# Two PSUM banks for the last projections and four for the level steps of a two-level attention layer

## The reference, cut to what matters

```python
q = silu(q); g = lb + (1 - lb) * sigmoid(f); k = 1 - g
b = cumsum(log(g))                       # within a chunk of tokens, per head and key
a[t, s] = sum_d q[t,d] * exp(b[t,d] - b[s,d]) * k[s,d]     # only s <= t
o = a @ i + (what earlier chunks left in the state)
o = rms_norm(o) * silu(gate);  y = o @ c_w_out
```

## Time and profile before

| | us |
|---|---|
| median of 3 runs | 1267.08 (1266.88 to 1267.08) |
| the profiled execution, its own time | 1267.41 |
| its span, first to last instruction | 1265.6 |
| PE busy | 1250.7 (99%) |
| DVE busy | 986.0 (78%) |
| ACT busy | 747.9 (59%) |
| DMA queue of the weights, share of 16 engines | 51.6% |

### The profile page before, as it was taken

How to read it: one execution, slowest core, us unless ns; L and a number is a source line. 1 busy time by engine, 2 the same in 40 slices (tenths; PEclk the granted TensorE clock), 3 DMA queues, 4 the chain that set the end, 5 groups by cost and what they waited for, 6 DMA issues and landing times.

```text
span 1265.6 us, 22039 instructions
## 1 busy us (share of the span) xinstructions
PE 1250.7 (99%) x8384; PEld 1095.7 (87%) x8384; DVE 986.0 (78%) x1476; ACT 747.9 (59%) x1135; POOL 17.8 (1%) x34
## 2 busy tenths in 40 slices
PE   9999999999999999999999999999999999999997
PEld 7898888888999988888888888888889897888886
DVE  5997899889798879998987676767676665867665
ACT  6565665555888766565557556444445645644443
POOL 0200000000000010000000000000000000000000
PEclk9999999999999999999999999999999999999999
DMA  9754555655544357555536344555655443655551
GB/s 297 262 167 150 183 167 199 199 196 170 167 134 143 127 185 261 200 178 189 199 104 222 118 139 154 200 183 184 198 194 172 134 146 121 216 183 184 199 195 38
DMA packets 165816, 223.16 MB, mean 176 GB/s; under 512 B 5224, under 2 KB 144624, under 8 KB 165616
## 3 DMA queue, kind: packets, MB, share of 16 engines
q1 hardware_dynamic: 163408, 216.04, 51.6%
q0 software_dynamic: 1904, 5.47, 1.3%
q10 hardware_dynamic: 432, 0.64, 0.1%
HBM read 221.08 MB, written 1.06 MB: 176 GB/s over the span
## 4 chain that ended last, share of the span: by engine, by line
PE 89%; DVE 5%; ACT 3%; issue 1%; DMA 1%; SPq 0%; DVEq 0%; ACTq 0%
PE bank L615 24%; PE bank L404 15%; PE bank L405 14%; PE bank L406 14%; PE bank L618 12%; DVE wlow L1707 1%; PE bank L709 1%; PE bank L745 1%; ACT whigh L1205 1%; PE bank L462 1%; PE bank L731 1%; PE bank L524 1%; DMA raw<-in_ab_w_in 1%; PE bank L465 1%; DVE h_e L2164 1%
## 5 line engine op out<-in xcount | busy, mean ns | idle before, releaser
L1707 DVE TENSOR_TENSOR wlow<-raw,whigh 128x2048 fp32r<-128x2048 f32 (+1 forms) x203 | 462.5, 2281 | 132.9 <-ACT whigh L1205 132.6
L1205 ACT ACTIVATE whigh<-raw 128x2048 fp32r<-128x2048 f32 x202 | 386.2, 1912 | 225.2 <-PE bank L406 144.9
L615 PE MATMUL bank<-xn,whigh 128*128 128x512 f32 x1312 | 328.1, 392 | 0.0
L615 PEld LDWEIGHTS bank<-xn,whigh 128*128 128x128 f32 x1312 | 238.1, 189 | 44.2
L618 PEld LDWEIGHTS bank<-xn,wlow 128*128 128x128 f32 x1312 | 179.0, 190 | 12.8
L618 PE MATMUL bank<-xn,wlow 128*128 128x256 f32 x1312 | 182.9, 282 | 0.0
L404 PE MATMUL bank<-xn,whigh 128*128 128x256 f32 (+1 forms) x496 | 142.6, 288 | 0.2 <-DVE f_mk L2287 0.2
L405 PE MATMUL bank<-xn,whigh 128*128 128x256 f32 (+1 forms) x496 | 140.2, 283 | 0.0
L406 PE MATMUL bank<-xn,wlow 128*128 128x256 f32 (+1 forms) x496 | 140.2, 283 | 0.0
L404 PE MATMUL bank<-whigh,g_high 128*128 128x512 f32 (+1 forms) x356 | 138.6, 389 | 0.2 <-DVE g_low L1903 0.2
L405 PE MATMUL bank<-wlow,g_high 128*128 128x512 f32 (+1 forms) x356 | 138.1, 388 | 0.0
(11 more groups left out here) (305 smaller groups left out, 1723.3 us busy)
## 6 DMA issues: line engine op xcount, KB each, us to landing
raw<-in_ffn_w_up SPq DMA_DIRECT2D x44, 1024.0 KB, 5.1
raw<-in_w_gate_up SPq DMA_DIRECT2D x44, 1024.0 KB, 5.0
raw<-in_ffn_w_down SPq DMA_DIRECT2D x22, 1024.0 KB, 4.9
raw<-in_w_down SPq DMA_DIRECT2D x22, 1024.0 KB, 4.9
raw<-in_c_w_in SPq DMA_DIRECT2D x16, 1024.0 KB, 5.6
raw<-in_ab_w_in SPq DMA_DIRECT2D x14, 1024.0 KB, 6.5
raw<-in_w_in_fox SPq DMA_DIRECT2D x10, 1024.0 KB, 5.3
raw<-in_w_in_moba SPq DMA_DIRECT2D x10, 1024.0 KB, 5.1
```

The lines of the kernel that those rows point to most:

```text
L615: pe.matmul(o[:, :].rearrange("p (h t) -> p h t", h=2), wh[:, k, j * P:(j + 1) * P], xn[:, :, k, :], start=k == 0, stop=False)
L1205: act.activation(whigh[s][:, 0:w], raw[s][:, 0:w], ACT.Copy).then_inc(w_high, 1)
L1707: dve.tensor_tensor(wlow[s][:, 0:w], raw[s][:, 0:w], whigh[s][:, 0:w].bitcast(F), ALU.subtract).then_inc(w_low, 1)
```

## The change

From unit 13 on the projections' ring has two banks, 0 and 1, and the level steps have four, 2, 4, 5, 3, from step 24 on. The lag is four steps again from there. The steps that stood in the middle of units 13 and 14 go to the ends of these units: unit 13 had one in its middle (24) and three at its end (25, 26, 27), unit 14 two (28, 29) and two (30, 31); each has four at its end now. Unit 15 keeps one in its middle (32) and three at its end. The first two rows of the output's bank order are adapted, and DVE picks one step more in unit 15.

```diff
-LEVEL_GROUPS = {4: (0, 2), 5: (0, 2), 6: (0, 2), 7: (0, 3), 8: (0, 2), 9: (0, 2), 10: (0, 3), 11: (0, 3), 12: (0, 3), 13: (1, 2), 14: (2, 2), 15: (1, 2)}
+LEVEL_GROUPS = {4: (0, 2), 5: (0, 2), 6: (0, 2), 7: (0, 3), 8: (0, 2), 9: (0, 2), 10: (0, 3), 11: (0, 3), 12: (0, 3), 13: (0, 3), 14: (0, 4), 15: (1, 2)}
...
-    OUT_BANKS = {0: (1, 6, 7, 0), 1: (1, 2, 0, 3), 2: (0, 1, 6, 7), 3: (0, 1, 7, 6)}
+    OUT_BANKS = {0: (1, 6, 7, 0), 1: (0, 2, 1, 3), 2: (0, 1, 6, 7), 3: (0, 1, 7, 6)}
...
-    WIDE_LEVELS = 21
+    WIDE_LEVELS, FOUR_BANKS = 21, 24
...
         if i < WIDE_LEVELS:
             return 3 + i % 5
-        return {32: 4, 33: 5, 34: 4, 35: 3}.get(i, 3 + (i + 1) % 3)
+        return 3 + (i + 1) % 3 if i < FOUR_BANKS else (2, 4, 5, 3)[i % 4]
...
-        lag = lambda n: 4 if n < WIDE_LEVELS + 2 else 3
+        lag = lambda n: 3 if WIDE_LEVELS + 2 <= n < FOUR_BANKS else 4
...
                 name, j = HGRN_UNITS[u]
+                if u == 13:
+                    ring_banks[0] = (0, 1)
                 unit = unit_columns if name in "fq" else unit_tokens
...
             if u == 15:
                 heads_low(0)
-                for i in range(ALL_STEPS - 3, ALL_STEPS):
+                for i in range(ALL_STEPS - 4, ALL_STEPS):
                     pick(i)
```

## The result

| | us |
|---|---|
| before, median of 21 runs | 1267.24 (1266.84 to 1267.53) |
| after, median of 21 runs | 1269.57 (1267.99 to 1269.90) |
| ratio after / before | 1.0016, interval 1.0010 to 1.0022 |
| the profiled execution of after, its own time and span | 1269.69, 1267.9 |

The change costs 2.3 us, and the interval lies wholly above 1. The ratio is within the 0.2% that the prediction counted as no change. The prediction's 1267.08 times the ratio is 1269.1, under the range's top of 1269.3; the median itself, 1269.57, lies 0.27 above that top. The 21 times stand in two groups with nothing between them: 7 from 1267.99 to 1268.59, with the median 1268.17, and 14 from 1269.33 to 1269.90, with the median 1269.66. The lower group is the forecast of 1268.2; the other lies 1.5 us above it. The profiled execution belongs to the upper group.

What follows compares the result with a forecast made beforehand. PE was taken to bound the kernel, busy 1250.7 of 1265.6 us. Unit 15 starting 1.68 us later, less 0.55 at step 32, gives +1.13 on 1267.41, so 1268.5, or a median of 1268.2; range 1266.0 to 1269.3.

Steps and rivals of the forecast that it cites:

- Part 1: Units 13 and 14: fewer changes between projections and level steps save PE 0.43 us, bounds 0.2 and 0.6.
- Part 2: Step 32: with four step banks it uses bank 2, so PE's wait there goes, -0.55 us.
- Part 3: Unit 15's start: PE waits 2.1 us for ACT to empty bank 1; the unit starts 1.68 us later.
- the signs named ahead as showing the prediction wrong: Unit 15's idle time missing, under 1 or over 3 us; granted clock behind it under 1.00; new PE wait elsewhere.
- The sum: Whole kernel: unit 15's 1.68 us later start less step 32's 0.55 gives +1.13 us, median 1268.2.
- the rival of the clock: Behind unit 15's new wait the granted clock falls; half a unit at half pace costs 2.9 us, 1271.1; chance 0.10.
- The new wait does not come: Unit 15: ACT has unit 13's result out by 428.34, leaving only the savings, -0.98 us, 1266.1; chance 0.08.
- given back later: After unit 15: later PE waits shrink and return the delay, giving 1267.1; chance 0.04.

Runs made afterwards that it cites:

- the lumps alone: The kernel before with only the table of groups changed, level steps in fours at the ends of units 13 and 14: 1271.98 us, ratio 1.0038.
- the short lag: The changed kernel with ACT taking unit 13's result behind step 31's exponentials, and a lag of three steps instead of four: 1271.33 us, ratio 1.0029.
- the ring alone: The kernel before with only the projections' two-bank ring from unit 13 on and the output's bank order changed: 1270.06 us, ratio 1.0019.
- the first experiment: The changed kernel, but ACT takes unit 13's result earlier, behind step 31's exponentials: 1265.99 us, ratio 0.9991 against the kernel before.
- the longer wait: The changed kernel with two unread 128x512 copies on ACT ahead of unit 13's result: 1271.09 us, ratio 1.0032 against the kernel before.

## Why the prediction was right, and where it was not

**Part 1** was right: step 24 and unit 14 within 0.08 us of the times worked out; the lumps save 0.44 to 0.54 (forecast 0.43, bounds 0.2 and 0.6), and unit 14 is 0.20 shorter in the trace (420.71 to 428.26 against 421.02 to 428.77, forecast 0.19). The prediction took for granted that the picks' new place brings PE no wait. That holds for the changed kernel, and the lumps alone and the short lag show what it hangs on: `low` ahead of the pick.

**Part 2** was right: step 32's wait is gone. With the old places and no new wait the kernel is 0.66 under the one before (forecast 0.55).

**Part 3** was right in mechanism and size: wait 2.16 (2.1), ended by `h_i`, 0.58 earlier than before (0.55). Taking the wait away gives 1268.17 - 1265.99 = 2.18, or 0.93 + 1.10 = 2.03 with each against the kernel before that ran beside it. Of the signs named ahead as showing the prediction wrong, one came: a granted clock under 1.00 behind this wait.

**The sum** of the three, +1.13, gives the lower group: 1268.17 against 1267.24 is +0.93. From unit 13's start to step 32 the traced execution of that group takes 433.31 - 413.36 = 19.95 us, the one of before 432.45 - 413.60 = 18.85: +1.10, so the sum holds where it was worked out.

**Luck.** The forecast of 1268.2 describes 7 of 21 runs. That 1269.1 falls under the range's top of 1269.3 is luck: the top was set for a longer chain on ACT, and what brought the median up to it was the lower clock, which the range left out.

**The step that was mis-sized is the rival of the clock**, in both its numbers. Its chance was put at 0.10, and the median fell into it: 14 of 21 runs, 6 of 11 with the ring alone. Its price was put at 2.9, a half unit at half pace, and it measured 1.5: the pace came back to 0.36 after five groups (431.25 to 434.45), not after eight, and a group took 0.64 at the lower clock, not 0.72. The range left this case out at 1271.1; at its measured price the median lies only 0.27 above the range's top. The step of the argument that failed is the weighing of the wait between 1.55 us without a lower clock and the kernel's end with one: the 2.1 us were taken to lie with the former, and in two of three runs they lay with the latter. The groups are told apart by their times; two executions of the upper one and one of the lower were traced, and all three show what their group should. The Trainium skill's page "TensorE: Matmul & The Clock Gate", in "Why this matters for your kernels", warns against idle gaps between bursts of matmuls that are longer than this one. By that the clock would have stayed: so it did in 7 runs, in the other 14 it fell, and the measurement decides.

**The rivals that fell.** "The new wait does not come" and "given back later" both fell: unit 16's first matmul starts at 441.33 in the profiled execution, 438.80 in that of before, and of these 2.53 us 2.3 are in the span (1267.9 against 1265.6). Transfers as the cause of the slow pace fell with the first experiment, and with the lower group's trace, where the DMA share is 0.98 and the clock 1.00.

**Left open:** what decides in one execution whether a wait of 2.16 us lowers the clock, and why 3.5 us came at two prices. The last two traces of the changed kernel, one of each group, are alike to 0.02 us at unit 13's start (413.38 and 413.36) and at the restart (430.26 and 430.24), and no run here tells more.

## What to carry to other kernels

With one bank fewer in a ring, the engine that fills it waits for the engine that empties it, and how long depends on where that engine's own program order puts the emptying: look there first, and move the emptying into that engine's idle time before shrinking the ring (here +2.3 us became -1.1, with the same two instructions). When a change trades buffers for reordering, test the order of all streams that the lag governs: the same lumps cost 4.9 us when the pick stood ahead of `low`. And price a new wait of PE of about two microseconds twice, with and without the clock, and take times that stand in two groups as a sign of it.

## What the runs showed of the hardware that was not expected

A wait of PE of 2.16 us brought the granted clock to 0.50 in some executions of one and the same program and left it at 1.00 in others; single waits of 0.36, 0.62, 1.53 and 1.56 us have no lower clock behind them in the traces read, nor has the 2.03 us of the short lag's, but 0.45 and 1.50 close together have one with the lumps alone. Behind the 2.16 us the pace fell only after PE had gone on (at 431.25 where PE restarted at 430.42), so that the cost appears in matmuls that wait for nothing; behind the 3.52 us of the longer wait it was down from the first matmul. The end of the kernel is no measure of it either. In the trace of before, the clock is on the way down in 1260 to 1262, where the last matmul ends at 1259.06; in that of after the last one starts at 1261.06, and the stretches read:

```profile
1262.00:1264.00 2.00, 0.00 (x0) 0.00 (x0) 1.97 (x6) 1.65 (x7) 0.00 (x0) 1.00 0.00 0
1264.00:1266.00 2.00, 0.00 (x0) 0.00 (x0) 0.78 (x2) 0.72 (x1) 0.00 (x0) 0.51 0.87 323
```

The clock was still whole where it had been falling before at the same distance. The row at the end, on which the rival's condition was built, differs from one execution to the next.
